# Order of the exp and value matmuls in the attention loop of a hybrid encoder block

## What is computed

```python
def mla_attention(q_nope, q_rope, k_nope, k_rope, v):
    ...
        s = (jnp.einsum('bqhd,bkhd->bhqk', qn_b, k_nope)
             + jnp.einsum('bqhr,bkr->bhqk', qr_b, k_rope))
        p = jax.nn.softmax(s.astype(jnp.float32) * ATTN_SCALE, axis=-1).astype(v.dtype)
        return jnp.einsum('bhqk,bkhd->bqhd', p, v)
```

## Time and profile before

| what | value |
|---|---|
| time before, median of 2 runs | 2029.47 us (2017.41 and 2041.53) |
| the profiled execution: its own time | 2020.22 us |
| its span on the slowest core (core 7) | 2018.4 us |
| spans of the 8 cores | 1980.5 to 2018.4 us |
| TensorE busy / ScalarE busy on core 7 | 1438.4 us (71%) / 758.8 us (38%) |
| mean granted TensorE clock, core 7 | 0.861 of full speed |

### The profile page before, as it was taken

One profiled execution on the slowest core, in us unless ns is written; L12 is line 12 of the kernel. 1 busy time (PEld: TensorE's weight loads), 2 busy tenths in 40 slices (PEclk: granted clock), 3 DMA queues, 4 the chain that ended last, 5 costly groups with the idle time before them and its releaser, 6 DMA issues.

```text
span 2018.4 us, 20614 instructions; the slowest of 8 cores (1980.5 to 2018.4 us)
## 1 busy us (share of the span) xinstructions
PE 1438.4 (71%) x6300; PEld 592.0 (29%) x6300; DVE 573.1 (28%) x838; ACT 758.8 (38%) x1045; POOL 101.1 (5%) x161
## 2 busy tenths in 40 slices
PE   0165266526665879798688979778897977888895
PEld 0122122213231223343222334322233432233342
DVE  5621112022211323331432323233232323224133
ACT  0344223313523651622465271256427125743201
POOL 2200310300200000000000000000000000000000
PEclk9986587767987889899888989978898988889898
DMA  9929991990895004455501634440153442015343
GB/s 96 167 60 139 98 142 38 104 145 17 94 104 117 1 11 138 131 141 132 153 1 32 156 113 136 135 133 0 34 164 106 136 132 91 1 49 168 110 141 104
DMA packets 137993, 200.46 MB, mean 99 GB/s; under 512 B 63408, under 2 KB 68656, under 8 KB 136944
## 3 DMA queue, kind: packets, MB, share of 16 engines
q0 software_dynamic: 62944, 67.41, 24.4%
q1 hardware_dynamic: 74944, 131.74, 23.2%
HBM read 232.96 MB, written 36.96 MB: 134 GB/s over the span
## 4 chain that ended last, share of the span: by engine, by line
PE 60%; ACT 14%; DMA 11%; DVE 6%; issue 5%; another core or an unknown queue 2%; POOL 1%; ACTq 0%; DVEq 0%; POOLq 0%; SPq 0%
PE psb L462 31%; PE psb L802 9%; DMA wbuf<-w_ada 7%; ACT U L718 6%; PE psb L708 4%; PE psb L723 4%; PE psb L609 4%; PE psb L766 3%; PE psb L732 2%; ACT hT L496 2%; DVE hT L492 1%; ACT sq L474 1%; ACT U L731 1%; ACT U L730 1%
## 5 line engine op out<-in xcount | busy, mean ns | idle before, releaser
L462 PE MATMUL psb<-hT,wbuf 128*128 128x512 bf16 x2272 | 538.6, 399 | 87.7 <-ACT hT L496 63.8
L462 PEld LDWEIGHTS psb<-hT,wbuf 128*128 128x128 bf16 x2272 | 227.5, 102 | 392.4 <-issue 158.3
L718 ACT ACTIVATE U<-psb 128x1024 bf16<-128x1024 f32 x256 | 253.9, 1022 | 130.4 <-PE psb L708 129.7
L802 PE MATMUL psb<-wbuf,U 128*128 128x512 bf16 x960 | 217.8, 385 | 35.2 <-DVE nrm_tmp L524 15.3
L723 PE MATMUL psb<-U,vaug 128*66 128x512 bf16 x512 | 172.3, 421 | 68.1 <-ACT U L718 68.1
L708 PE MATMUL psb<-U,kT 96*128 96x512 bf16 x512 | 169.2, 416 | 2.1 <-DVE U L528 2.1
L831 ACT ACTIVATE sig<-psb 128x512 f32<-128x512 f32 x88 | 52.4, 597 | 265.8 <-PE psb L462 154.0
L348 PE MATMUL psb<-caT,wbuf 128*128 128x1 bf16 x384 | 16.8, 165 | 189.9 <-DMA wbuf<-w_ada 189.9
L802 PEld LDWEIGHTS psb<-wbuf,U 128*128 128x128 bf16 x960 | 93.3, 99 | 159.1 <-issue 57.5
L833 DVE TENSOR_TENSOR U<-psb,sig 128x512 bf16<-128x512 f32 x88 | 60.8, 691 | 238.7 <-PE psb L462 217.2
L609 PE MATMUL psb<-zz,U 128*128 128x512 bf16 x496 | 114.5, 394 | 15.6 <-ACT zz L638 13.5
(11 more groups left out here) (139 smaller groups left out, 1263.2 us busy)
## 6 DMA issues: line engine op xcount, KB each, us to landing
wbuf<-scr_wd SPq DMA_DIRECT2D x121, 256.0 KB, 2.8
wbuf<-scr_win SPq DMA_DIRECT2D x108, 256.0 KB, 2.8
wbuf<-scr_wg SPq DMA_DIRECT2D x88, 256.0 KB, 2.7
wbuf<-scr_wu SPq DMA_DIRECT2D x88, 256.0 KB, 2.7
wbuf<-scr_wout SPq DMA_DIRECT2D x64, 256.0 KB, 3.5
wbuf<-w_ada POOLq DMA_DIRECT2D x48, 256.0 KB, 14.7
xg<-x POOLq DMA_DIRECT2D x24, 512.0 KB, 32.4
scr_win<-w_in_c POOLq DMA_DIRECT2D x9, 768.0 KB, 21.7
```

The source lines that it names most:

```text
L462: sc.op(pe, lambda e, o=o, k=k, lhs=lhs, kw=kw: e.matmul(o, lhs(k), rhs_fn(k), start=(k == 0), stop=(k == nk - 1), **kw), reads=[wb_] + rh ...
L718: sc.op(act, lambda e, pt=pt, j=pbs[0] // 2: e.activation(out=pt.rearrange("p a n -> p (a n)"), in_=PSB[j][:, :], func=AF.Exp, scale=ATTN_ ...
L802: sc.op(pe, lambda e, wfl=wfl, k=k, j=j, hf=hf, pb=pb: e.matmul(bank(pb), lhs_fn(k, j), wfl[:, hf * 512:(hf + 1) * 512], start=(k == 0), s ...
```

## The change

`EP_pair` is split into `E_pair` and `P_pair`. The loop runs over the 64 steps of a group as one row, and each turn issues S of the next step, E of this one, and P of the step *before*. `P_pair(h, 7)` is thereby issued in the first turn of the next head. The tail of the head before is still issued in the turn kp = 1, and `q_head` in the turn kp = 3. The second matmul of every P pair now raises TensorE's semaphore. `NPT` stays 2, and so do the banks.

**Queue order on TensorE after:** S(k+1), P(k-1), S(k+2), P(k), ... with the tail's matmul behind P0 and `q_head` behind P2.

```diff
-            def EP_pair(h, kp):
+            def E_pair(h, kp):
                 pbs = (0, 1) if kp % 2 == 0 else (2, 3)
+                pi_ = (h * 8 + kp) % NPT
+                pt = pT[pi_]
+                sc.op(act, lambda e, pt=pt, j=pbs[0] // 2: e.activation(out=pt.rearrange("p a n -> p (a n)"), in_=PSB[j][:, :],
+                                                                       func=AF.Exp, scale=ATTN_SCALE),
+                      reads=[PB[pbs[0]], PB[pbs[1]]], writes=[buf("pT%d" % pi_)])
+
+            def P_pair(h, kp):
                 po = 4 + (h % 2)
                 pi_ = (h * 8 + kp) % NPT
                 pt = pT[pi_]
                 ptb = buf("pT%d" % pi_)
-                sc.op(act, lambda e, pt=pt, j=pbs[0] // 2: e.activation(out=pt.rearrange("p a n -> p (a n)"), in_=PSB[j][:, :],
-                                                                       func=AF.Exp, scale=ATTN_SCALE),
-                      reads=[PB[pbs[0]], PB[pbs[1]]], writes=[ptb])
                 for i in range(2):
                     kt = kp * 2 + i
                     sc.op(pe, lambda e, h=h, kt=kt, i=i, pt=pt, po=po: e.matmul(bank_rows(po, 0, 66), vaug[:, kt, h, :], pt[:, i, :],
                                                                                start=(kt == 0), stop=(kt == 15)),
-                          reads=[buf("vaug"), ptb], writes=[PB[po]], ms=(kt == 15))
+                          reads=[buf("vaug"), ptb], writes=[PB[po]], ms=(i == 1))
...
             S_pair(0, 0)
             pending = None
-            for h in range(NH):
-                for kp in range(8):
-                    if kp < 7:
-                        S_pair(h, kp + 1)
-                    elif h + 1 < NH:
-                        S_pair(h + 1, 0)
-                    EP_pair(h, kp)
-                    if kp == 1 and pending is not None:
-                        tail(pending)
-                        pending = None
-                    if kp == 3 and h + 1 < NH:
-                        q_head(h + 1, g)
-                pending = h
-            tail(pending)
+            for it in range(NH * 8):
+                h, kp = divmod(it, 8)
+                if it + 1 < NH * 8:
+                    S_pair(*divmod(it + 1, 8))
+                E_pair(h, kp)
+                if it >= 1:
+                    hp, kpp = divmod(it - 1, 8)
+                    P_pair(hp, kpp)
+                    if kpp == 7:
+                        pending = hp
+                if kp == 1 and pending is not None:
+                    tail(pending)
+                    pending = None
+                if kp == 3 and h + 1 < NH:
+                    q_head(h + 1, g)
+            P_pair(NH - 1, 7)
+            tail(NH - 1)
```

## The result

The changed kernel is slower: the ratio to the kernel before, measured beside it, is 1.0142 with a 95% interval of 1.009 to 1.0194. On a median of 2016.3 us for the kernel before that is +29 us (18 to 39); the median of the changed kernel is 2051.9 us. The ratio leaves out executions in which some of the cores ran slower at a lower granted clock; the two medians include them. The change costs less than 2%, where the forecast was +15 (7 to 27).

The account below looks back on a forecast made before the run. Attention was taken as bound by a 2.35 us latency loop, neither TensorE nor ScalarE full. Three groups' 4.1 us each (12) plus 3 in the other gave +15 on 2020.2: 2035 us, range 2005 to 2060.

Parts of the forecast that it names:

- Part 1: Regular steps of a head: S and P swap places, the loop stays at 2.35 us, gain 0.
- The rival that the `pT` wait doesn't bind: Regular loop of a head: 0.43 us go in every loop of 2.35, -41 us, 1979; chance 0.02.
- the two readings weighed there: Regular loop's gaps: too few tile copies, so 2.35 us stays; or the order is the cause, giving 1.92 us.
- Part 2: One more semaphore increment on 224 P pairs: between 0 and 0.01 us a pair, taken as 0.
- Parts 3 and 4: Full-clock head: P1 behind the tail loses 0.5 us, `q_head` in a hole repays it; 12.14 instead of 12.27 us.
- Part 5, the price of a stretch: Heads partly at half clock: a stretch costs 1.69 us above the full-clock head, against 1.13 before.
- Part 5, the number of stretches: Half-clock stretches per group: 6 after, from 5, 5, 9 and 5; +4.1 us in three groups, +3 in the other.
- The step to the kernel's time: Whole kernel: the attention's +15 us added to the profiled execution's 2020.2 us gives 2035.
- The rival "the clock holds": Attention heads: `q_head` fills a gap, the clock falls less often, -8 to -30 us, 1990 at the end; chance 0.11.

Follow-up runs that it names:

- the filled kernel: Changed kernel with seven unread score matmuls added ahead of the tail's matmul, where TensorE idles 1.63 us; ratio 0.9798 to the kernel before.
- the filler runs: Unread score matmuls put ahead of the tail's matmul: seven in the changed kernel, ratio 0.9798; three in the kernel before, ratio 0.9841.

## Why the forecast was right, and where its size was off

- **Part 1 (regular steps, gain 0): shown.** The loop is 2.35 us in both orders. Three tiles free it in the new order (1.93) and do nothing in the old one. The rival that the `pT` wait doesn't bind is thereby out. One sentence there was too wide: that a tile with too few copies ends these gaps holds for the new order only. In the old one a third tile changes nothing, since S stands behind P in TensorE's queue. The loop falls only with the new order and the third tile together, so neither of the two readings weighed there was right alone.
- **Part 2 (semaphores, 0): shown** by the run with them alone.
- **Parts 3 and 4 (full clock, 12.14 us a head, 10.10 for the last): shown.** 12.15 and 10.10 us in the filled kernel. The gap of 1.7 (by TensorE's own ends 1.63) came as worked out.
- **Part 5, the price of a stretch (1.69): shown**, 1.65 by the heads of 13.80. The prediction raised it from 1.13 because P3 comes to stand behind `q_head`. That is borne out: with `q_head` put back behind P3 a stretch costs 1.12, with P1 put back it still costs 1.6. P1 in its new place makes every head 0.4 to 0.5 us longer, slow or not; at full clock the new place of `q_head` pays that back (part 4), in a slow head it doesn't.
- **Part 5, the number of stretches: the term that was too small.** I took 6 a group. The clock of core 7 shows seven in each of the four groups, one of them long, so that no head escapes. The groups' 95.6 us less 82.9, divided by 1.65, give the same, 7.7. The first, second and fourth group cost 6.6 each on average instead of 4.1, which makes 20 instead of 12. The third group cost 2.2 where I took 3, close by luck: I had read nine stretches from its excess, and the clock before shows six, one of them long. They lie later in the head and cost mostly 1.4 to 1.7 us, not 1.13. Hence +21.8 instead of +15 in the attention.
- The step to the kernel's time: the ratio gives +29 (18 to 39). What exceeds 22 us lies within its interval, and no stage of the trace shows it as an effect of the change. The profiled execution's 2053.6 us is no witness for the forecast of 2035, as 30 us of it are the low clock of the last part.
- **The rival "the clock holds"** had the sign of the effect wrong for this order, but its mechanism exists: with the gap filled the clock does hold, and 50 us return, more than the whole order is worth.
- Of the two rules of the Trainium skill that were weighed, the first (Perfetto Trace Analysis, Identifying the Most-Contended Engine), that bubbles that repeat can come from too few buffers, held for the new order, shown by the third tile; in the old order the same gap of 0.41 us had another cause. The second (TensorE: Matmul & The Clock Gate, on psum-queue depth-cycling), that frequent idle times between groups of matmuls let the clock swing, agrees with the filler runs: with the tail's gap filled the granted clock is 1.00 in all groups. The regular gaps alone didn't make it fall there, but beside the gap at the tail they count, as the table shows.

Left open: what makes the clock fall, the length of one gap or the idle time of a head in sum, and why one stretch per group lasts twice as long. On core 7 of the changed kernel the clock falls 1.6 to 3.9 us behind a head's logarithm, and the four long stretches are the four that begin earliest in their head, by 2.2 us at the latest.

## What to carry to other kernels

Moving a consumer one step later in a pipeline gains nothing when its input buffer is reused at the same distance: count the copies first, since the freed wait comes back as the wait for the buffer. And ask of each insert in the loop (a tail, a projection) what used to fill the hole it makes; here putting back one value pair of a head's eight took the whole loss away. In this kernel a hole on TensorE was paid a second time by the clock after it, so the order to look for is the one that fills the longest hole with work that must be done anyway.

## What the runs showed of the hardware that I had not expected

- Seven matmuls that nobody needs, in one gap of 1.63 us a head, made the kernel faster by 3.4% of its time (ratios 1.0142 and 0.9798), by keeping the granted clock at 1.00 through the heads.
- At full clock most heads repeat to 0.01 us from one to the next and from core to core, so 0.13 us a head could be read in single executions, where the whole kernel's time scatters by over 1%.
- In one execution of the changed kernel two cores ran their last 260 and 262 us at a mean granted clock of 0.79 where core 0 had 0.90, with tens of us on end at 0.81: on core 7 30 us more than in the kernel before, with no difference in the program's work there.
- The same gap of 1.22 us at the tail goes with 28 stretches at half clock in one kernel and 13 in another, whose other gaps are closed.
